# Ending the first layer's mixer block by block, with weight strips placed between recurrence steps

## What is computed

```python
def even_mixer(x, w_in, ...):
    p = x @ w_in
    y_a = rwkv7_mix(p[..., :RWKV_COLS], ...)      # recurrence, head norm, bonus, gate g
    y_b = mlstm_mix(p[..., RWKV_COLS:], ...)      # decayed linear attention, head norm, sigmoid(o) gate
    return jnp.concatenate([y_a, y_b], -1) @ w_out

def peer_ffn(x, w_q, sub_k1, sub_k2, u_tab, v_tab):   # per block of 128 tokens
    q = (xb @ w_q).reshape(T, 8, 2, 128)              # scores of 2 x 128 keys, top 16 of each, top 16 of 256 sums
    act = gelu(einsum('td,thkd->thk', xb, u_tab[eid]))
    return einsum('thk,thkd->td', gate * act, v_tab[eid])
```

## Time and profile before

| what | value |
|---|---|
| median of three runs | 1781.21 us |
| the profiled execution: its own time | 1780.13 us |
| its span, first to last instruction | 1777.7 us |
| TensorE, VectorE, ScalarE, GpSimd busy | 87%, 60%, 34%, 32% of the span |
| mean granted TensorE clock | 0.969 of 2.4 GHz |
| chain that ended last, by engine | TensorE 52%, DMA 34%, ScalarE 6%, VectorE 6% |
| moved by DMA | 638.3 MB, of which 536.9 MB are the gathers |

### The profile page before, as it was taken

The page is one execution under the profiler, slowest core; times in us unless marked ns, Lnnn a source line. Parts: engine busy times, 40 slices in busy tenths (PEclk is TensorE's granted clock), DMA queues, the critical chain, the costliest instruction groups (busy, mean ns, idle before and its releaser), DMA issues.

```text
span 1777.7 us, 18617 instructions
## 1 busy us (share of the span) xinstructions
PE 1538.4 (87%) x6020; PEld 921.1 (52%) x6020; DVE 1062.2 (60%) x2499; ACT 604.7 (34%) x1759; POOL 576.6 (32%) x561
## 2 busy tenths in 40 slices
PE   8999988999877778998899978998999968777776
PEld 7779977764322225763456525663457523222222
DVE  1584634577888875334556447665556468874444
ACT  1434411233333333227532323346632323332222
POOL 2000000244444442233432442334432444443441
PEclk9999958999999999999999999999999999999999
DMA  6222003899999999999999999999999999999996
GB/s 250 96 74 93 1 1 111 342 411 427 426 427 427 426 427 422 427 426 427 427 424 425 421 427 425 427 426 427 427 382 426 397 426 427 427 427 427 427 427 275
DMA packets 92063, 638.32 MB, mean 359 GB/s; under 512 B 11072, under 2 KB 13120, under 8 KB 15424
## 3 DMA queue, kind: packets, MB, share of 16 engines
q0 software_dynamic: 73728, 536.90, 71.8%
q1 hardware_dynamic: 18240, 100.24, 14.4%
HBM read 636.05 MB, written 1.05 MB: 358 GB/s over the span
## 4 chain that ended last, share of the span: by engine, by line
PE 52%; DMA 34%; ACT 6%; DVE 6%; issue 3%; POOL 1%; ACTq 0%; SPq 0%; POOLq 0%; DVEq 0%
DMA arena<-l_peer_uv,arena 33%; PE psum L905 22%; PE psum L587 14%; PE psum L886 5%; DVE arena L1715 3%; PE psum L764 2%; PE psum L809 1%; PE psum L680 1%; PE psum L670 1%; PE psum L679 1%; ACT L1202 1%; POOL arena L554 1%; ACT arena L1207 1%; ACT early L1215 1%; ACT arena L1215 1%
## 5 line engine op out<-in xcount | busy, mean ns | idle before, releaser
L554 POOL DMA_INDIRECT arena<-l_peer_uv,arena x512 | 563.4, 1100 | 1089.3 <-PE psum L905 828.9
L1715 DVE CUSTOM_DVE_ANT_0 arena<-arena,xres 128x1024 f32<-128x1024 f32 x512 | 619.3, 1223 | 406.5 <-DMA arena<-l_peer_uv,arena 400.9
L905 PE MATMUL psum<-arena,early 128*128 128x512 f32 x1024 | 477.6, 611 | 99.8 <-ACT early L1215 96.4
L905 PE MATMUL psum<-arena 128*128 128x512 f32 x1024 | 474.5, 608 | 95.7 <-ACT arena L1215 92.2
L905 PEld LDWEIGHTS psum<-arena,early 128*128 128x128 f32 x1024 | 189.4, 193 | 359.5 <-issue 200.4
L905 PEld LDWEIGHTS psum<-arena 128*128 128x128 f32 x1024 | 189.1, 192 | 354.8 <-issue 210.4
L587 PE MATMUL psum<-xT,wring 128*128 128x128 f32 (+2 forms) x1856 | 295.9, 319 | 12.5 <-DMA wring<-l_w_in 8.2
L587 PEld LDWEIGHTS psum<-xT,wring 128*128 128x128 f32 (+1 forms) x1856 | 268.5, 191 | 51.6 <-issue 21.1
L1202 ACT ACTIVATE arena<-arena 128x2 f32<-128x2 f32 x256 | 52.0, 203 | 595.4 <-DVE arena L1715 595.1
L1030 ACT COPY arena<-psum 128x256 f32<-128x256 f32 (+2 forms) x138 | 62.5, 472 | 220.8 <-PE psum L587 117.3
L1207 ACT ACTIVATE arena<-arena 128x1 f32<-128x1 f32 x512 | 123.3, 287 | 23.8
(11 more groups left out here) (236 smaller groups left out, 1142.7 us busy)
## 6 DMA issues: line engine op xcount, KB each, us to landing
wring<-l_w_in SPq DMA_DIRECT2D x47, 1024.0 KB
wring<-l_peer_wq SPq DMA_DIRECT2D x24, 1024.0 KB
wring<-l_w_out SPq DMA_DIRECT2D x12, 1024.0 KB
arena<-l_peer_uv,arena POOLq DMA_INDIRECT x512
ln_par<-l_ln_g SPq DMA_DIRECT2D x6, 512.0 KB
ln_par<-l_ln_b SPq DMA_DIRECT2D x6, 512.0 KB
arena<-l_peer_keys SPq DMA_DIRECT2D x2, 1024.0 KB, 6.9
xT<-x_t SPq DMA_DIRECT2D x1, 1024.0 KB, 4.8
```

What stands on the lines that cost most here:

```text
L554: pool.indirect_dma_start(out=ring[:, g % RING, :], out_offset=None, in_=T[f"l{l}_peer_uv"], in_offset=bass.IndirectOffsetOnAxis(ap=eid[:, ...
L905: last = mm(self.ps[c], diag[k % DIAGS], ring[:, g % RING, D + c * 512:D + (c + 1) * 512], start=not self.begun, stop=True, skip_group_che ...
L1715: v.tensor_tensor_reduce(out=u, in0=u, in1=xres[:, self.b, :], scale=1.0, scalar=0.0, op0=ALU.mult, op1=ALU.add, accum_out=hid[:, self.b, ...
```

## The change

- **Gate rows and values.** The two gate rows are projected by one matmul group, 36 columns wide, in place of two groups of 4. The mLSTM values are projected with the tokens as stationary operand (`value_strip`), so that they come out by token and need no transposes (`mv_turn` goes). Only the two value strips stay ahead of the inversion.
- **Output-gate strips.** The two strips for the mLSTM's output gate are projected in halves between the steps of the first two chunks (`gate_half`).
- **Gate-row arithmetic.** `mlstm_rows` and the SiLU move on VectorE from ahead of the inversion to after its second and third level; their Exp and Ln (`decay_logs`, `row_exp`) move on ScalarE to the same places. `Tc`, the scratch of the inversion, lies at another address.
- **End by block.** The head norms are made for each token block by itself, and the output projection is made for block 0 first (its mLSTM half around the last chunk's `seq_u`), then for block 1. Block 0's LayerNorm, its first query and key scores and the routing of its first head come before block 1's last projection and LayerNorm (`finish_block`).
- **Loads.** All four output strips are resident at once, the fourth in a borrowed piece of the arena, and a copy of the first query strip is loaded into another borrowed piece, so that this strip is loaded twice. The next strips wait for `mix_out` 2. The gather ring has the same ten places in another order, and the seventh gather waits for `mix_out` 3 as well.
- **PEER.** TensorE handles the first pair of expert rows ahead of the third head's query (it was after that of the fourth), and two more after it; buffers behind the ring are permuted.

```diff
-        add_strips("l0_w_in", M0 + 4 * MW, M0 + 4 * MW + 2 * MH, "gates_in", 0, 1)
-        add_strips("l0_w_in", M0 + 2 * MW, M0 + 4 * MW, "vo_in", 0, 1)
-        add_strips("l0_w_out", 0, D, "mix_out", 0, 1)
+        strips.append((T["l0_w_in_rest"].rearrange("p (k n) -> p k n", k=KT), GATE_COLS, "gates_in", 0))
+        add_strips("l0_w_in", M0 + 2 * MW, M0 + 3 * MW, "v_in", 0, 1)
+        add_strips("l0_w_in", M0 + 3 * MW, M0 + 4 * MW, "o_in", 0, 1)
+        out_strip = len(strips)
+        add_strips("l0_w_out", 0, D, "mix_out", 2, 0.5)
+        query_strip = len(strips)
+        add_strips("l0_peer_wq", 0, STRIP, "peer_q", 0, 1)
...
+        borrowed = {LAST_OUT: cut(28160, KT * STRIP), query_strip: cut(0, KT * STRIP)}
...
+                    if i == LAST_OUT:
+                        await_filled(sp, "inv_d", 4 * len(LEVELS) - 1)
+                    elif i == query_strip:
+                        await_filled(sp, "seq_s", 2)
+                    elif turn_of[i] >= WRING:
+                        before = strips[in_turn[turn_of[i] - WRING]]
+                        await_filled(sp, before[2], before[3])
+                    sp.dma_start(strip_buffer(i)[:, :, 0:w], src).then_inc(strip_loaded(i), 16)
...
-            load_strips(16 + WRING - 3)
-            await_filled(sp, "seq_y", NCH - 1)
+            load_strips(16 + 4 - 3)
+            await_filled(sp, "seq_y", 1)
             load_keys(0)
-            load_strips(6 - WRING)
+            load_strips(1 + 2)
...
+                    if g == EARLY_ROWS:
+                        await_filled(pool, "mix_out", 3)
...
+                def value_strip(t):
+                    w = next_strip(pe)
+                    ps = claim(pe, "v_in", t)
+                    for b in range(NB):
+                        for k in range(KT):
+                            last = mm(ps[:, b * STRIP:(b + 1) * STRIP], xT[:, k, b * P:(b + 1) * P], w[:, k, :],
+                                      start=(k == 0), stop=(k == KT - 1))
+                    done(last, "v_in")
...
-                project(ps[0:MH, 0:SEQ], w, 0, MH)
-                done(project(ps[0:MH, SEQ:2 * SEQ], w, MH, MH), "gates_in")
-                for t in range(4):
-                    w = next_strip(pe)
-                    ps = claim(pe, "vo_in", t)
-                    for q in range(2):
-                        last = project(ps[:, q * SEQ:(q + 1) * SEQ], w, P * q, P)
-                    done(last, "vo_in")
+                done(project(ps[0:GATE_COLS, 0:SEQ], w, 0, GATE_COLS), "gates_in")
+                for t in range(2):
+                    value_strip(t)
...
+                pe.wait_ge(S("silu"), 2)
...
+                def gate_half(t, q):
+                    if q == 0:
+                        gate_strips[t] = next_strip(pe)
+                    ps = claim(pe, "o_in", t)
+                    last = project(ps[:, q * SEQ:(q + 1) * SEQ], gate_strips[t], P * q, P)
+                    if q == 1:
+                        done(last, "o_in")
...
+                for c in range(NB):
+                    chunk_x(c)
+                    gate_half(c, 0)
+                    chunk_u(c)
+                    gate_half(c, 1)
+                    chunk_state(c)
+                    chunk_y(c)
+                    if c == 0:
+                        pe.wait_ge(S("v_in_taken"), 2)
+                    values(c)
+                chunk_x(2)
+                turn_heads("h_turn", h_tok, 0, "h_normed")
+                chunk_u(2)
+                chunk_state(2)
+                chunk_y(2)
+                turn_heads("y_turn", y_tok, 0, "y_normed")
+                out_strips = [next_strip(pe) for _ in range(4)]
+                def project_out(b, tiles, ks, first, end):
+                    for i in tiles:
+                        ps = claim(pe, "mix_out", 2 * b + i)
+                        for q in range(2):
+                            for k in ks:
+                                last = mm(ps[:, q * STRIP:(q + 1) * STRIP], yT[:, k, b * P:(b + 1) * P],
+                                          out_strips[2 * i + q][:, k, :], start=first and (q, k) == (0, ks[0]),
+                                          stop=end and (q, k) == (1, ks[-1]), skip_group_check=True)
+                        if end:
+                            done(last, "mix_out")
+                m_half, r_half = range(RT, KT), range(0, RT)
+                chunk_x(3)
+                turn_heads("h_turn", h_tok, 1, "h_normed")
                 pe.wait_ge(S("h_mixed"), 1)
-                begun = []
-                for i in range(WRING):
-                    if i == WRING - 1:
-                        for b in range(NB):
-                            turn_heads(2 + b, y_tok, b, "y_normed", 1 + b)
-                    w = next_strip(pe)
-                    ps = claim(pe, "mix_out", i)
-                    project_out(ps, w, range(RT, KT), True, False)
-                    begun.append((ps, w))
+                project_out(0, (0,), m_half, True, False)
+                chunk_u(3)
+                project_out(0, (1,), m_half, True, False)
+                chunk_state(3)
+                chunk_y(3)
                 pe.wait_ge(S("mixed"), 1)
-                for ps, w in begun:
-                    done(project_out(ps, w, range(0, RT), False, True), "mix_out")
-                w = next_strip(pe)
-                done(project_out(claim(pe, "mix_out", WRING), w, range(0, KT), True, True), "mix_out")
+                project_out(0, (0, 1), r_half, False, True)
+                pe.wait_ge(S("h_mixed"), 2)
+                project_out(1, (0, 1), m_half, True, False)
+                turn_normed(0)
+                pe.wait_ge(S("x_turn_taken"), 2)
+                queries(0, next_strip(pe), slice(0, P))
+                turn_heads("y_turn", y_tok, 1, "y_normed")
+                pe.wait_ge(S("keys_loaded"), 16)
+                pe.wait_ge(S("peer_q_taken"), 1)
+                scores(0, 0, [0])
+                pe.wait_ge(S("mixed"), 2)
+                project_out(1, (0, 1), r_half, False, True)
+                turn_normed(1)
...
+                def decay_logs():
+                    act.wait_ge(S("m_abs"), 1)
+                    st.then(af(mr[0:MH, 3, :], mr[0:MH, 3, :], ACT.Exp, scale=-1.0))
+                    st.settle()
+                    af(mr[0:MH, 3, :], mr[0:MH, 3, :], ACT.Ln, bias=ONE[0:MH]).then_inc(S("m_log"), 1)
+                def row_exp():
+                    act.wait_ge(S("m_neg"), 1)
+                    af(mr[0:MH, 5, :], mr[0:MH, 5, :], ACT.Exp).then_inc(S("m_rows"), 1)
...
+                    if i == 1:
+                        decay_logs()
+                    if i == 2:
+                        row_exp()
...
+                take_seq_x(0)
+                take_seq_u(0)
+                take_seq_x(1)
+                h_root(1, 0)
+                take_seq_u(1)
+                take_gate(0)
+                take_gate(1)
+                y_root(2, 0)
+                take_seq_x(2)
+                turned("h_turn", 0)
+                take_seq_u(2)
+                h_root(3, 1)
+                turned("y_turn", 0)
+                take_seq_x(3)
+                turned("h_turn", 1)
+                take_seq_u(3)
                 ln_root(0)
-                ln_root(1)
...
+                y_root(4, 1)
...
                 take_x(0, 0)
                 queries(0, 0, slice(0, P))
+                turned("y_turn", 1)
+                scores(0, 0, [0])
+                gate_exp(0, *FIRST_GROUPS[0])
+                ln_root(1)
                 take_x(2, 1)
...
+                    if i == 1:
+                        mlstm_silu()
+                    if i == 2:
+                        mlstm_rows()
...
+                def finish_block(b):
+                    for i in range(2):
+                        x = xres[:, b, i * 512:(i + 1) * 512]
+                        if (b, i) == (0, 0):
+                            dve.wait_ge(S("x_loaded"), 16)
+                        taken(stt(x, x, ALPHA, full(dve, "mix_out", 2 * b + i), ALU.mult, ALU.add), "mix_out")
+                        dve.wait_ge(S("mix_out_taken"), 2 * b + i + 1)
+                        half_stats(b, i)
+                    layer_norm(b, 2)
+                chunk_state(0)
+                chunk_y(0)
+                mlstm_values(0)
+                h_norm(1, 0)
+                chunk_state(1)
+                chunk_y(1)
+                y_norm(2, 0)
+                mlstm_values(1)
+                h_norm(3, 1)
+                chunk_state(2)
+                gate_heads(0)
+                chunk_y(2)
+                mix_heads(0)
+                gate_heads(1)
+                chunk_y(3)
+                finish_block(0)
+                y_norm(4, 1)
+                mix_heads(1)
+                route(0, 0, FIRST_GROUPS[:1], lambda g, i: None)
+                finish_block(1)
...
+            ex.pairs(2)
+            route(0, 0, FIRST_GROUPS[1:], meanwhile)
...
```

(46 more changed lines are left out.)

310 lines of the change are left out of this document (141 added, 169 removed).

## The result

The changed kernel takes **1788.26 us** (median of six runs, 1785.65 to 1790.87), the kernel before 1781.49 on the same chip (six runs, 1778.16 to 1782.22): a ratio of 1.0044, interval 1.0032 to 1.0055. I had forecast 1773 and faster; it is slower, and just above my range. The profiled execution took 1790.33, its span is 1788.6.

The account below looks back on a forecast made before the run. The end was taken as the first gather's time, DMA units behind it and DMA idle time, with TensorE a limit alongside. -25.0 + 7.4 + 9.2 = -8.4 from 1780.1 gave 1771.7, with 1.1 for the median 1773; range 1757 to 1787.

Parts of the forecast that it names:

- the inversion's +6.3: Inversion: moved row arithmetic on ScalarE makes TensorE wait between levels, +6.3 us, between 0 and 7.9.
- the wait for `row_exp`: Inversion: `row_exp` waits for VectorE's rows, so evictions start later and `inv_d` waits some 3.4 us.
- The upper bound, 7.9: Inversion: the most the moved row arithmetic would add, 7.9 us, if none of it were covered.
- the 310: First gather, forecast near 298: one after 310 us would show the prediction wrong.
- The scores: Between inversion and first recurrence step: the `mv_turn` transposes go, -1.0 us.
- The start: Ahead of the inversion: fewer matmul records, so it begins at 134.6 instead of 151.8 us, -17.2.
- The recurrence: Up to chunk 3's start: 47.5 us against 45.2 before, mostly full clock, +5 for half clock late.
- Rival 3: Recurrence and block 0's projection: half clock also during the strips makes the kernel slower, halfway 1787 us; chance 0.13.
- +7.4: Behind the first gather: parameters and two query strips, three units of DMA, now follow it, +7.4 us.
- +9.2: Behind the first gather: TensorE frees rows late, so DMA engines lack work, +9.2 us, bounds 0 and 18.
- Three gaps: Behind the first gather: DMA below 427 GB/s in three or four holes, 40 to 80 us after it.
- -8.4: Whole kernel: sum of the earlier gather, -25.0, and the terms behind it, +7.4 and +9.2: -8.4 us.

Follow-up runs that it names:

- e6: e1 with VectorE's rows and the last Exp (`row_exp`) put back between inversion levels, after the third: 1778.49 us, 0.999 of the kernel before.
- e1: The changed kernel with the gate-row arithmetic on ScalarE and VectorE moved ahead of the inversion: 1762.24 us, 0.9886 of the kernel before.
- e4: e1 with the output-gate strips projected ahead of the inversion again, not between recurrence steps: 1770.54 us, 0.9946 of the kernel before.
- e11: e1 with one Ln on an unused ScalarE row between the second and third inversion levels: 1784.35 us, 1.0018 of the kernel before.
- e8: e1 with the third head's query ahead of the first expert rows, and 28 unread matmuls while TensorE waits for block 1's norm: 1766.44 us.

## Why the prediction was wrong, step by step

Positions in the profiled executions, as the prediction's steps give them and as after shows them:

| step | predicted | after |
|---|---|---|
| inversion starts | 134.6 | 137.14 |
| inversion lasts | 57.1 | 75.6 |
| from there to the first recurrence step | 5.1 | 9.6 |
| recurrence up to chunk 3 | 47.5 | 41.8 |
| from there to block 0's product | 26.8 | 25.8 |
| from there to the first gather | 27.2 | 26.1 |
| first gather | 298.3 | 316.07 |
| from the first gather to the end of the span | 1471.0 | 1472.5 |

The rows of after that the steps come from, TensorE, VectorE and GpSimd in time (119.65: the gate rows; 264.11: chunk 3; 289.95: block 0's product is full):

```profile
119.65 3.64 PE L607 MATMUL psum<-xT,wring 128*36 128x256 f32 x16
123.23 14.08 PE L619 MATMUL psum<-wring,xT 128*128 128x256 f32 x64
264.11 0.47 PE L869 MATMUL psum<-arena 64*64 64x64 f32 x2
289.95 0.69 DVE L1724 SCALAR_TENSOR_TENSOR xres<-xres,psum 128x512 f32<-128x512 f32 x1 [1.97 <-PE psum L812]
316.07 1.14 POOL L574 DMA_INDIRECT arena<-l_peer_uv,arena  x1 [220.35 <-DVE arena L1814]
```

**The step that failed is the inversion's +6.3.** The waits themselves came about as I had them: the step of `decay_logs` took 3.5 us and TensorE waited 2.53 where I had 2.9 (my own rows give 175.6 + 3.5 + 1.05 - 177.7 = 2.5); the wait for `row_exp`, 3.4 in my sum, is 2.87 in e6, and did not come in after, at half clock. The error was to price a wait as its length. I had written the clock's behaviour into the recurrence, and for the inversion carried over the 1.00 of the earlier trace rows as if it belonged to the work; it belonged to work whose only gap was 0.32 us. The upper bound, 7.9, was a bound on idle time only. The term was about 25 us, +18.5 over mine. The range would have needed a case in which the wait costs the clock, and the rows for it were there: some 25 us of inversion at full clock lie behind that wait, and the earlier trace rows show one instruction group at either level, 1.11 and 1.94 us; that ratio makes 19 us more of them. The first gather, at 316.07, lies past the 310 that the prediction named as a sign of being wrong.

**The scores** added 4.5 us, and only part of that is the wait's. I had taken over the time of before less 1.0 for the transposes. From the inversion's end to the first recurrence step it is 5.1 as forecast, 8.2 in e1 (184.83 to 193.02), whose scores fall to half clock with no wait ahead of them, and 9.6 in after. So 3.1 us are a second miss of the same kind, the clock of before carried over to changed work, and 1.4 are what the inversion left behind.

**The start** was 17.2 us of work less as priced: one 3.64 us group and two strips in 14.08 against 34.89. It lies 2.5 us late because an earlier stage that the change leaves alone, the small projections at 62 us, ran slower in this execution; in e1 the same code had the inversion start at 134.77. The rows show the clock at work there too. The same 24 records behind the same wait, in before, after and e4:

```profile
61.76 7.57 PE L611 MATMUL psum<-arena 64*128 64x256 f32 x24 [2.89 <-ACT arena L1058]
62.71 9.33 PE L641 MATMUL psum<-arena 64*128 64x256 f32 x24 [2.89 <-ACT arena L1108]
62.11 4.86 PE L641 MATMUL psum<-arena 64*128 64x256 f32 x24 [2.89 <-ACT arena L1112]
```

In after the clock is 0.50 from 62 to 72 us, in e4 it is 1.00. At this place, then, a wait of 2.89 us cost the clock in some executions and not in others; what decides it was not tried.

**The recurrence** was better than forecast: strips held 1.00 through chunks 0 and 1 and it fell to 0.50 from 260 on, in chunk 2, as predicted, but only for some 13 us. e4 shows the strips' part. Rival 3 ended on the right side of the result for a wrong reason: there was no half clock during the strips.

**Behind the gather** I had +7.4 and +9.2, 16.6 together, over the 1454.4 us of before; measured is 18.1. Three gaps stand where predicted, 45, 60 and 75 us after the first gather, in the table by stage of after (last column GB/s):

```profile
361.00:366.00 5.00, 5.00 (x17) 2.58 (x17) 4.86 (x18) 4.49 (x14) 1.57 (x2) 1.00 0.89 280
376.00:381.00 5.00, 5.00 (x15) 2.34 (x15) 3.96 (x16) 4.41 (x14) 1.88 (x2) 1.00 0.85 275
391.00:396.00 5.00, 5.00 (x13) 2.13 (x13) 4.93 (x17) 4.52 (x19) 2.24 (x2) 1.00 0.82 256
```

How the 18.1 us divide between more transfers and missing traffic stands less firmly: mean rates of 418 and 416 GB/s over the two stretches, rounded, give some 11 and 7 us, each uncertain by about 2.

**The sum.** With every step as measured it is -8.4 + 18.5 + 4.5 - 5.7 - 1.0 - 1.1 + 1.5 = +8.3 us, and 2.5 for the late start: +10.8; the spans differ by 10.9. Without the 18.5 of the inversion and the 1.4 that it left to the scores it would have been -11.6, and e1, whose inversion takes 50.06 us and so spares the 6.3 of waits as well, has a span 17.0 shorter than before. The other steps were right enough that this one decided the sign.

## What to carry to other kernels

In a stage like this inversion, in which TensorE is busy without a gap at 2.4 GHz, the price of a wait can be the rest of the stage at 1.2 GHz and not its length: here 0.80 us cost 22, and 0.32 nothing. Before moving work of another engine into such a stage, find its slack there to a tenth of a microsecond, move it ahead of the stage, or give TensorE something to do meanwhile. And a stage that holds the full clock in the trace of before does not promise it to a kernel that puts a wait into it.

## What the runs showed of the hardware

**A short wait inside the inversion cost the clock for the rest of it.** In after, matmuls of 64 columns kept 1.00 up to the wait (160 to 162 us: 2.00 busy of 2.00) and then had 0.50 for 58 us at 57.21 us busy. The same work thus runs at either level, by what came before it. In e11 one wait of 0.80 us was enough; in before one of 0.32 us was not.

The Trainium skill (TensorE: Matmul & The Clock Gate, Part 1, HAM oscillation — how this bites in real kernels) tells of TensorE falling to half clock in DMA waits of some microseconds, and the table of states above it gives the full clock back to an array that is kept busy. Here the fall came with far less idle time, 0.80 us in e11, and an array busy 57.21 of 58.00 us stayed at half clock; the measurement decides. The Trainium skill (TensorE: Matmul & The Clock Gate, Part 1, A second HAM failure mode: psum-queue depth-cycling) also tells of a clock that oscillates where TensorE idles often and briefly between groups of matmuls. That is nearer to what e11 shows, though there they recur and here one was enough.

**The clock can also come back soon.** In e8, behind 6.4 us of matmuls without a gap, waits of 0.59 and 1.16 us on either side of 1.09 us of transposes were followed by 0.50 from 296 to 298 us; from 299 on it was 1.00, after some 3 us of query matmuls of 128 columns.
